# The first layer's gates computed inside the mixers' first turn, and the first quad's weights split in the setup block

## The reference

```python
proj = h @ w_in
qg, kg, vg, zg, ag, qm, km, vm, om, zm, im, fm = _split(proj, AB_SPLITS)
gate = jax.nn.log_sigmoid((ag @ gla_w_a2 + gla_b_a).astype(F32)) / GLA_GATE_TEMP
...
logf = jax.nn.log_sigmoid(fg)            # mLSTM: fg = fm + ml_b_f, ig = im + ml_b_i
...
fcum = jnp.swapaxes(jnp.cumsum(lfc, axis=1), 1, 2)
m_i = jnp.maximum(inter, jnp.max(dlog, axis=-1))
```

## Time and profile before

| | us |
|---|---|
| three runs | 2224.47, 2226.04, 2227.22 |
| median | 2226.04 |
| the profiled execution's own time | 2225.12 |
| its span, first to last instruction | 2223.7 |
| `setup`, to PE's last matmul of it | about 52 |
| `gates0`, to PE's first projection | about 52 to 87 |
| `ab_mixers`, to PE's end of it | about 87 to 1253 |
| layer 1 | the rest |

### The profile page before, as it was taken

The page is one execution under the profiler, slowest core; times in us unless marked ns, Lnnn a source line. Parts: engine busy times, 40 slices in busy tenths (PEclk is TensorE's granted clock), DMA queues, the critical chain, the costliest instruction groups (busy, mean ns, idle before and its releaser), DMA issues. The chain is left out here.

```text
span 2223.7 us, 41532 instructions
## 1 busy us (share of the span) xinstructions
PE 2101.4 (95%) x15171; PEld 1965.8 (88%) x15171; DVE 1417.5 (64%) x2602; ACT 1006.0 (45%) x1516; POOL 276.9 (12%) x419
## 2 busy tenths in 40 slices
PE   6699999999999999999999599999999999989997
PEld 4599999898989899898999599889888989879996
DVE  4554737475648475585654557787788778875544
ACT  3444444443334343343343346456465475564432
POOL 1100102020101102020100101221211312210000
PEclk8699999999999999999999799999999999999998
DMA  3664667584947758496875175665665766756851
GB/s 96 209 181 139 216 215 261 162 303 145 298 120 222 225 155 283 117 309 209 295 232 183 57 219 171 196 202 175 200 197 171 208 190 186 211 201 193 281 162 68
DMA packets 337147, 436.97 MB, mean 197 GB/s; under 512 B 17644, under 2 KB 296732, under 8 KB 335584
## 3 DMA queue, kind: packets, MB, share of 16 engines
q1 hardware_dynamic: 298672, 298.96, 44.3%
q0 software_dynamic: 38144, 136.48, 18.2%
q10 hardware_dynamic: 224, 0.05, 0.0%
HBM read 355.35 MB, written 80.06 MB: 196 GB/s over the span
## 5 line engine op out<-in xcount | busy, mean ns | idle before, releaser
L145 PE MATMUL bank<-xn_hi,w_hi 128*128 128x288 f32 x3584 | 1079.3, 301 | 35.0 <-ACTq L996 12.3
L146 PE MATMUL bank<-xn_lo,w_hi 128*128 128x288 f32 x3584 | 1060.6, 296 | 0.0
L147 PE MATMUL bank<-xn_hi,w_lo 128*128 128x288 f32 x3584 | 1058.1, 295 | 0.0
L132 DVE TENSOR_TENSOR w_lo<-w_raw,w_hi 128x1024 fp32r<-128x1024 f32 x512 | 624.7, 1224 | 628.3 <-ACT w_hi L126 618.8
L126 ACT ACTIVATE w_hi<-w_raw 128x1024 fp32r<-128x1024 f32 x512 | 541.6, 1060 | 942.1 <-PE bank L147 850.4
L145 PEld LDWEIGHTS bank<-xn_hi,w_hi 128*128 128x128 f32 x3584 | 676.0, 189 | 61.1 <-issue 35.6
L146 PEld LDWEIGHTS bank<-xn_lo,w_hi 128*128 128x128 f32 x3584 | 677.2, 189 | 5.6
L147 PEld LDWEIGHTS bank<-xn_hi,w_lo 128*128 128x128 f32 x3584 | 677.8, 189 | 0.0
L1224 DVE SCALAR_TENSOR_TENSOR state<-state,decay,bank 128x512 f32<-128x512 f32 x128 | 92.1, 740 | 0.0
L1827 POOL DMA_DIRECT2D out_ssm_s<-ssd_state x64 | 48.0, 756 | 305.5 <-DVE ssd_state L2255 242.2
L2094 ACT ACTIVATE ssd_state<-ssd_state,ssd_we 128x128 f32<-128x128 f32 x256 | 82.5, 415 | 0.0
(11 more groups left out here) (441 smaller groups left out, 2339.4 us busy)
## 6 DMA issues: line engine op xcount, KB each, us to landing
w_raw<-in_w_in_ab SPq DMA_DIRECT2D x224, 512.0 KB, 3.8
w_raw<-in_w_in_c SPq DMA_DIRECT2D x128, 512.0 KB, 4.2
w_raw<-in_w_out_ab SPq DMA_DIRECT2D x64, 512.0 KB, 4.7
w_raw<-in_w_out_c SPq DMA_DIRECT2D x64, 512.0 KB, 3.8
state<-in_state_gla POOLq DMA_DIRECT2D x32, 512.0 KB, 9.9
out_gla_s<-state POOLq DMA_DIRECT2D x32, 512.0 KB, 4.2
state<-in_state_mlstm_c POOLq DMA_DIRECT2D x32, 512.0 KB, 10.0
out_mc_s<-state POOLq DMA_DIRECT2D x32, 512.0 KB, 5.4
```

What stands on the lines that cost most here:

```text
L132: dve.tensor_tensor(core.w_lo[:, j], core.w_raw[:, j % RAW], core.w_hi[:, j].bitcast(F32), ALU.subtract).then_inc(ws["split"], 1)
L145: pe.matmul(banks[m][:, 0:T], core.w_hi[:, j, kk, col], hi[:, k], start=f, stop=False)
L146: pe.matmul(banks[m][:, 0:T], core.w_hi[:, j, kk, col], lo[:, k], start=False, stop=False)
L147: ins = pe.matmul(banks[m][:, 0:T], core.w_lo[:, j, kk, col], hi[:, k], start=False, stop=e)
```

## The change

Two things change.
1. **The split of quad 0 moves to `setup`.** SP issues its four loads right behind the input's, ACT copies to `w_hi` between the norm's root and the copies to `xn_hi` (the new argument `then` of `scalar_r`), and DVE subtracts to `w_lo` after its last `xn_lo`.
2. **The block `gates0` is gone.** Its work is now the class `Gates0`, whose methods are called within the first turn of `ab_mixers` (where `sml is None`), at fixed pairs (i, j). The gates' product goes to bank 7, the eight products use banks 4 to 6 in turn, and the stores and the wait for them move from SP to POOL, ahead of `load_gates`. POOL's state loads wait for `done`, since the gates' buffers lie where the states will be.

```diff
@@ setup
+            for j in range(UNITS):
+                sp.dma_start(core.w_raw[:, j], wq[:, UK * j:UK * j + UK, 0:GW]).then_inc(ws["arrived"][j], 16)
...
             norm.vector(dve, core.bank[4], st)
+            dve.sem_inc(ws["split"], RAW)
+            split_lo(dve, core, ws, 0)
...
-            norm.scalar_r(act, st)
+            act.sem_inc(ws["used"], UNITS)
+            norm.scalar_r(act, st, lambda: split_hi(act, core, ws, 0))
@@ class Gates0
+    def gpsimd(self, pool):
...
+        pool.wait_ge(self.gc_d, 8)
+        pool.dma_start(scr["gcum"], self.au[:]).then_inc(self.saved, 16)
+        pool.wait_ge(self.saved, 64)
...
+    def scalar(self, act, at, st):
+        if at == (0, 0):
+            act.wait_ge(self.fu_d, 1)
...
+        if at == (0, 3):
+            act.wait_ge(self.u_d, 8)
...
+    def tensor(self, pe, at):
+        if at in ((0, 0), (0, 1)):
+            pe.wait_ge(self.ag_d, 1)
+            pe.wait_ge(self.s_in, 64)
+            for t in ((0, 1, 2, 3), (4, 5, 6, 7))[at[1]]:
+                if t >= 3:
+                    pe.wait_ge(self.u_d, t - 2)
+                pe.matmul(B[4 + t % 3][:, 0:T], self.wa[:, t * P:(t + 1) * P], self.agT[:], start=True, stop=True
+                          ).then_inc(self.gps, 1)
+        if at == (0, 3):
...
+        if at == (1, 3):
...
+    def vector(self, dve, at, st):
...
+        if at in ((0, 0), (0, 1)):
+            for t in ((0, 1, 2, 3), (4, 5, 6, 7))[at[1]]:
+                dve.wait_ge(self.gps, t + 1)
+                dve.tensor_scalar(mn[:, t], B[4 + t % 3][:, 0:T], core.parT[:, C_BA + t:C_BA + t + 1], None, ALU.add
+                                  ).then_inc(self.u_d, 1)
...
+        if at in ((2, 0), (2, 1)):
+            for t in ((0, 1, 2, 3), (4, 5, 6, 7))[at[1]]:
+                dve.tensor_tensor_scan(au[:, t], core.keep[:], mn[:, t], 0.0, ALU.mult, ALU.add).then_inc(self.gc_d, 1)
@@ ab_mixers
+            g0.sync(sp)
             load_head(sp, 0, 0, 0, first=1)
...
+            g0.gpsimd(pool)
             load_gates(pool, 0)
+            pool_wait(pool, g0.done, 1)
             for b in range(NB):
                 load_state(pool, 0, 0, 0, b)
...
                             project_unit(pe, core, ws, q0 + i, j, core.xn_hi, core.xn_lo, 0, proj_banks[i % 2], True, True)
+                        if sml is None:
+                            g0.tensor(pe, (i, j))
...
                             split_lo_unit(dve, core, ws, q0 + i + 1, j)
+                        if sml is None:
+                            g0.vector(dve, (i, j), st)
```

More of the change, by code:

```diff
@@ L210, in tensor_sum, with scalar_r @@
                   skip_group_check=True).then_inc(self.sq_free, 1)
-    def scalar_r(self, act, steps):
+    def scalar_r(self, act, steps, then=None):
         act.wait_ge(self.var_ok, 1)
         rsqrt_act(act, self.r[:], self.var[:], steps).then_inc(self.r0, 1)
+        if then is not None:
+            then()
         if self.y is None:
@@ L399, in _ @@
             pe.wait_ge(gw_lo, 1)
-            gate_product(pe, core, gw[1], gw[2], core.bank[0][0:96, 0:T], norm.done, prod)
+            gate_product(pe, core, gw[1], gw[2], core.bank[7][0:96, 0:T], norm.done, prod)
 R_NM, R_EM, R_AL, R_M0, R_DEC, R_N = 0, T, 2 * T, 3 * T, 3 * T + TS, 3 * T + TS + NB
@@ L411, in layer0_buffers @@
                 nrow=sb("ml_n_rows", [NB, 4 * DK]), nT=sb("ml_nT", [P, 8, NB]))
[L414 to L470, removed]
-            for t in range(8):
[L472 to L482, removed]
-            for j in range(3):
[L484 to L489, removed]
-            st.then_wait(dve.tensor_scalar(big[:], core.keep[0:4, :], 1.0, 3.0e38, ALU.subtract, ALU.mult))
[L491 to L494, removed]
-            dve.tensor_scalar(ir[:], ir[:], bif[:, 0:1], None, ALU.add)
-            dve.tensor_scalar(fr[:], fr[:], bif[:, 1:2], None, ALU.add).then_inc(fu_d, 1)
-            for t in range(8):
-                b = core.bank[1 + t % 4][:, 0:T]
-                ba = core.parT[:, C_BA + t:C_BA + t + 1]
-                dve.wait_ge(gps, t + 1)
-                dve.tensor_scalar(mn[:, t], b, ba, None, ALU.add).then_inc(u_d, 1)
-            dve.wait_ge(fl_d, 1)
@@ L549, in ab_mixers @@
         vrow, krow = sb("v_rows", [P, 2, DV]), sb("k_rows", [P, 2, DK])
[L550 removed]
+        ahead = 4 * (12 * T + 2 * G_N + R_N + 6 * P + 416 + 2 * DV + 2 * DK)
+        skip = ahead - 4 * (2 * KT * T)
+        gap = 4 * (NB * 2 * DV + 4 * (3 + TP + NB * 7) + 4 * T + 4 * TS)
         state = sb("state", [P, NB, 2, DV])
@@ L581, in ab_mixers @@
         tmp.close()
+        with ExitStack() as over:
+            g0 = Gates0(core, sem, io, out, scr, g, over, ahead, gap)
         op = OutProj(core, sem, io, scr, ws, False, 0)
@@ L2381, in program @@
                 with nc.cleanup_on_exit():
-                    setup(nc, core, io, scr, gw)
-                with nc.cleanup_on_exit():
-                    gates0(nc, core, io, out, scr, g, ws)
+                    setup(nc, core, io, scr, ws, gw)
             with nc.cleanup_on_exit():
```

93 lines of the change are left out of this document (80 added, 13 removed).

## The result

The changed kernel takes 2212.33 us (median of four runs, 2209.83 to 2215.32) against 2225.68 for the kernel before beside it (four runs): a ratio of 0.9942, 95% interval 0.9929 to 0.9955, or 13.4 us less. The forecast was 19.0 us less, 2207.0, with a range of 2203 to 2211. The profiled execution took 2215.32 us, with a span of 2213.8.

The account below looks back on a forecast made before the run. PE's time was taken as the bound up to the first turn's end. Removing 34.7 and 1.85 us and adding 17.55 gave a gain of 19.0 us, hence 2207.0 us; range 2203 to 2211.

Parts of the forecast that it names:

- Block change: Between setup's last gate product and unit (0, 0): PE idle for 3.8 us, starting the unit at 55.81.
- First wait: After unit (0, 0), the fourth gate product waits for DVE's first addition: 6.3 us, bounds 4.8 to 8.3.
- Fourth and eighth product: The gate products that end the two waits in the first slot: 0.45 us each at full clock.
- Unit (0, 1) and the second wait: Unit (0, 1) ends at 69.0; then the eighth product waits 3.1 us for the fifth addition, to 72.1.
- Units (0, 2) and (0, 3): The last two units of the first slot run warm after the eighth product: 6.4 us.
- Transposes and the rest of the turn: 24 transposes after unit (0, 3), 1.33 us warm, and four at (1, 3), 0.25; together 1.6 us.
- The clock's own term: One cold restart of PE behind the first wait: 1.85 us, bounds 0 and 3.7.
- The clock stays low through the first slot: Rival: neither piece of PE's work wins the clock back, 7 us instead of 1.85; 2212 us, chance 0.11.
- the running sums come in time: At (4, 1), DVE's differences get the sums through POOL without a DMA wait; the rival of late sums had 0.04.
- the state loads cost PE nothing: States loaded in slots 3 and 4 beside weight loads: cost 0, at most 2.6 us.
- the early loads in setup do not hold up ACT: Quad 0's four loads in setup cost nothing: 9 us for 2 MB, needed by ACT only at 36.31.
- The waits hardly bite: Rival: quad 1's first two units are split as PE arrives, gain up to 25 us, 2201; chance 0.07.

Follow-up runs that it names:

- e_fill: Changed kernel plus 12 and 9 unread 128-row matmuls ahead of the fourth and eighth gate product, so PE multiplies while waiting; 2208.34 us.
- e_one: Changed kernel with DVE's additions ahead of quad 1's split at unit (0, 1) only; 2204.50 us.
- e_first: Changed kernel with DVE's additions ahead of quad 1's split at units (0, 0) and (0, 1); 2204.06 us.
- e_best: Changed kernel with additions ahead of splits, quad 0's low parts moved from setup's end to the mixers' start, and products spread 3, 3, 2; 2198.64 us.
- c_after: The changed kernel run again unedited; 2208.63 us, against the kernel before on the same chip 0.9898 to 0.9936.
- c_again: The changed kernel run once more unedited, on another chip; 2210.27 us, against the kernel before there 0.9921 to 0.9949.
- e_spread: Changed kernel with its eight gate products spread 3, 3 and 2 over units (0, 0), (0, 1) and (0, 2); 2197.76 us.

## Why the prediction was wrong

The mechanism of the two waits was right, and one term was too small: the clock. Step by step, in the prediction's order, with durations rather than moments, because setup was 1.2 us longer in this profile:

- **Block change.** From the last gate product to unit (0, 0): predicted 4.05 us (51.76 to 55.81), measured 3.80.
- **First wait.** From the start of unit (0, 0) to the fourth product: predicted 9.49, measured 9.24 (56.75 to 65.99). The load, the two splits and the addition came as worked out, and the low clock in unit (0, 0) did disappear in this wait. It left PE idle for 1.71 us where the prediction had 3 to 5, as unit (0, 0) took 5.82 us; the shorter gap did not make the restart behind it any cheaper.
- **Fourth and eighth product.** Predicted 0.45 each, measured 1.26 each. In e_fill, at the full clock, 0.68 passes from such a product (64.78) to the next unit (65.46), so 0.23 of each was undersized and 0.58 was the clock: the same product takes 1.32 us in after and 0.75 there.
- **Unit (0, 1) and the second wait.** Predicted 6.35, measured 8.69 (67.25 to 75.94), 2.34 more: the unit ran cold, and the second wait, which hangs on its end, moved with it.
- **Units (0, 2) and (0, 3).** Predicted 6.4, measured 9.05 (77.20 to 86.25), 2.65 more: (0, 2) cold.
- **Transposes and the rest of the turn.** 0.25 and 0.3 more.
- **The clock's own term.** 1.85, one cold restart, is to be set against 2 times 0.58, 2.34 and 2.65: 6.15.

The deviations add up to -0.25 - 0.25 + 2 times 0.81 + 2.34 + 2.65 + 0.25 + 0.3 - 1.85 = 4.8, which is 19.0 less 14.2. **The step that failed** is in "The clock": *"I take one restart in the cold behind it, 1.85; bounds 0 and 3.7"*. The upper bound failed as well. It was drawn from a single restart that had a long run of matmuls behind it, where the clock came back within 3.98 us. What the runs showed in its place are two such restarts, one behind each wait, at some 3.1 us each. In units (0, 1) and (0, 2) the matmuls keep the slow pace for 5.2 and 5.4 us (67.25 to 72.45, 77.20 to 82.64), so that only the last few of a unit run fast, and behind unit (0, 1) come narrow products and a wait that use the high clock for nothing.

That is the **rival** *"The clock stays low through the first slot"*, which had 0.11 and 2212: its terms were 2.6 for unit (0, 1), 1.4 for the products and up to 3 for the last two units, measured 2.34, 1.16 and 2.65. I had set against it that same restart, from one row of another situation. e_fill confirms the size of the term: with the additions as late as ever and most of the idle time filled, 6.0 us came back, against 6.15 by the list above; and in e_one a wait of 1.25 us was worth 4.5. What stays open is how much of it the idle time does and how much the narrow products beside it: in e_first the clock fell behind products alone. The Trainium skill, TensorE: Matmul & The Clock Gate, section Why this matters for your kernels, advises only against idle gaps that are longer than these; the measurement goes further, as the clock was at 0.54 and 0.52 behind gaps of 1.71 and 1.25 us with narrow products ahead of them.

**What was right.** That PE doesn't wait in slots 1 to 5 (80.00 busy of 80). That the running sums come in time: POOL's rows after are

```profile
114.24 0.58 POOL L461 DMA_DIRECT2D scr_gcum<-g_abs_u  x1 [20.61 <-DVE g_abs_u L551]
120.00 0.55 POOL L698 DMA_DIRECT2D head_rows<-scr_gcum  x1 [5.17 <-DMA scr_gcum<-g_abs_u]
```

and DVE's differences at 138.50 wait for no DMA. That the state loads cost PE nothing. That the early loads in setup do not hold up ACT: the four copies at 37.41 wait for no DMA. And that the gain carries through: the last matmul on `k_factor`, three turns on, is 13.0 us earlier (480.5 to 467.5), as is the first (178.3 to 165.3). *"The waits hardly bite"* was the picture of e_best rather than of this kernel: its interval is 25.2 us shorter, where that rival had up to 25.

**Beyond the interval.** In this profile 1.2 us went to a longer setup, and some 3 us to the later turns and layer 1, so that 9.9 us are left of 14.2 at the span's end; in c_after it was 16.4. Such differences come with an execution; the last section shows two. They move a single profile by as much as the error of the forecast, so the medians of c_after and c_again, 2208.63 and 2210.27, even lie in the forecast's range, which is luck and not the sum's merit; what shows the error of the sum is the interval, three times the same.

## What to carry to other kernels

When work that alternates with short waits is put into a stretch that TensorE bounds, price each piece of TensorE's work at the low clock until a row shows otherwise: taking away a wait of 1.25 us gave 3.0 and 4.5 us here. Then look at what stands ahead of the awaited instruction on the other engine's queue; placing the additions ahead of the split, or dealing out the products so that none needs an addition of its own step, took 7 to 10 us more than the change had. And before moving work out of a block's end, look for what lies beside it: the split alone, moved, gave nothing, as the block's end still waited for a store's landing.

## What the runs showed of the hardware

**Matmuls reach their full pace at different times in the same setup.** PE's pairs of 128-row matmuls on `su_sq` in setup, in after and in e_spread, whose instructions are the same up to there (start, duration):

```profile
23.05 1.33 PE L209 MATMUL bank<-su_sq,ones 128*128 128x288 f32 x2
24.91 0.75 PE L209 MATMUL bank<-su_sq,ones 128*128 128x288 f32 x2
```

```profile
13.70 0.75 PE L209 MATMUL bank<-su_sq,ones 128*128 128x288 f32 x2
```

PE begins at 6.15 and at 6.55 us and is busy throughout in both, and a pair takes 1.33 us up to there, yet the fast pairs come from 24.9 and from 13.7 on. The clock's column doesn't show this: it prints 1.00 over the slow pairs too (after, columns as above).

```profile
6.15:24.90 18.75, 18.75 (x52) 1.00 1.08 271
```

I take it for the clock all the same, since 1.33 and 0.75 are what two such passes of 288 columns take at the low and at the full clock (1.32 at 65.99 in after, 0.75 at 64.78 in e_fill). Over the thirteen profiles of the table the first fast pair lies between 13.20 and 26.34 us and setup's last gate product between 47.68 and 53.30, in the same order, with no edit ahead that would explain this.

**In the turns the clock falls for single moments, or doesn't.** In one of the later turns PE stands idle for a moment until ACT is done with a bank. First after, the matmul behind that idle time and the clock from there on, then c_after at the same place in its program (rows in order of time, and stretches as above):

```profile
714.14 0.57 PE L145 MATMUL bank<-xn_hi,w_hi 128*128 128x288 f32 x1 [2.02 <-ACT proj L953]
```

```profile
714.00:717.00 3.00, 2.86 (x12) 0.53 0.53 140
```

```profile
713.57 0.40 PE L145 MATMUL bank<-xn_hi,w_hi 128*128 128x288 f32 x1 [1.60 <-ACT proj L953]
```

```profile
713.00:716.00 3.00, 2.44 (x18) 1.00 0.59 161
```

After has three such falls in the mixers (also near 847 and 980 us), c_after none. From the last matmul on `k_factor` to the last on `k3m` after loses 1.5 us of its lead and c_after gains 3.8, on a kernel before that has three falls itself. The same kernel has three falls in one execution and none in another. e_fill's profile has three as well (near 537, 841 and 972 us) and loses against c_after's 3.8 us of its lead in that stretch; whether this is why their medians agree isn't shown.
